# Hybrid decoder trunk on one core: the SBUF addresses of the weight, activation and scratch tiles moved off multiples of 1,024 bytes

## The reference

```python
h = rms_norm(x, norm_w)
proj = h @ w_in                          # 2048 x (3072+1024+8+8+512+256+64+1024+2048+2048)
# mixer A, gated DeltaNet, 8 heads of 128: conv + SiLU + L2 norm on q, k; chunked delta rule
o_a = rms_norm(gated_delta_rule_chunked(q, k, v, g, beta), gdn_norm_w) * silu(z_a)
# mixer B, latent attention, 8 heads: low-rank q and kv, rotary key, causal softmax
o_b = causal_block_attention(q_full, k_full, v_b, scale) * silu(z_b)
merged = sigmoid(gate_a) * (o_a @ proj_a) + sigmoid(gate_b) * (o_b @ proj_b)
out = rms_norm(x + merged @ w_out, final_norm_w)
```

## The kernel before

| Tile | Before | Rest | After the change | Rest |
|---|---|---|---|---|
| const | 16,512 | 128 | 65,664 | 128 |
| param | 19,648 | 192 | 68,800 | 192 |
| gball | 21,056 | 576 | 74,304 | 576 |
| rec (x_c, state) | 21,312 | 832 | 226,112 (slot 30) | 832 |
| w_raw, w_hi, w_lo | 23,552 | 0 | 16,512 | 128 |
| krope, cs | 72,704 | 0 | 70,208 | 576 |
| h_hi, h_lo (and y) | 76,800 | 0 | 74,560 | 832 |
| c_hi, c_lo (and m_hi, m_lo) | 142,336 | 0 | 140,096 | 832 |
| slots | 166,912 | 0 | 164,672 | 832 |

## Time and profile before

### The profile page before, as it was taken

How to read it: one execution, slowest core, us unless ns; L and a number is a source line. 1 busy time by engine, 2 the same in 40 slices (tenths; PEclk the granted TensorE clock), 3 DMA queues, 4 the chain that set the end, 5 groups by cost and what they waited for, 6 DMA issues and landing times.

```text
span 1589.7 us, 21230 instructions
## 1 busy us (share of the span) xinstructions
PE 1546.0 (97%) x7380; PEld 1268.6 (80%) x7380; DVE 724.4 (46%) x1320; ACT 569.1 (36%) x1027; POOL 94.8 (6%) x166
## 2 busy tenths in 40 slices
PE   5999999899999999999999999999999999999997
PEld 2777887688888888888888888888887788888886
DVE  6626565654353453452552542543533544533332
ACT  4336566533333332333332432333333322222222
POOL 3000000000000000100000000000011110100000
PEclk8999999999999999999999999999999999999999
DMA  5222323221331321322322223313234544362222
GB/s 208 97 96 80 133 106 125 100 93 54 114 110 66 132 106 66 132 79 99 125 77 100 100 79 106 119 53 115 82 114 154 182 145 156 134 238 106 91 94 106
DMA packets 32390, 177.67 MB, mean 112 GB/s; under 512 B 4896, under 2 KB 4896, under 8 KB 16496
## 3 DMA queue, kind: packets, MB, share of 16 engines
q1 hardware_dynamic: 19872, 134.09, 23.8%
q0 software_dynamic: 12496, 43.30, 7.5%
HBM read 156.37 MB, written 21.00 MB: 112 GB/s over the span
## 4 chain that ended last, share of the span: by engine, by line
PE 94%; DVE 3%; DMA 1%; ACT 1%; issue 0%; SPq 0%; POOL 0%; DVEq 0%; ACTq 0%; POOLq 0%
PE bank L233 23%; PE bank L235 23%; PE bank L234 22%; PE bank L1414 4%; PE bank L1413 4%; PE bank L1415 4%; PE bank L1196 3%; PE bank L1186 3%; PE bank L1204 1%; PE bank L1348 1%; PE bank L1205 1%; PE bank L1133 1%; DMA slots<-in_xt 1%; DVE slots L712 1%; DVE h_lo L717 1%; DMA o_in<-o_scratch 1%
## 5 line engine op out<-in xcount | busy, mean ns | idle before, releaser
L233 PE MATMUL bank<-h_hi,w_hi 128*128 128x512 f32 x1520 | 633.0, 416 | 14.5 <-DVE h_lo L717 8.7
L235 PE MATMUL bank<-h_hi,w_lo 128*128 128x512 f32 x1520 | 596.9, 393 | 0.0
L234 PE MATMUL bank<-h_lo,w_hi 128*128 128x512 f32 x1520 | 595.7, 392 | 0.0
L225 DVE TENSOR_TENSOR w_lo<-w_raw,w_hi 128x512 fp32r<-128x512 f32 x468 | 306.1, 686 | 205.2 <-ACT w_hi L218 205.2
L233 PEld LDWEIGHTS bank<-h_hi,w_hi 128*128 128x128 f32 x1520 | 287.8, 189 | 84.1 <-issue 12.4
L234 PEld LDWEIGHTS bank<-h_lo,w_hi 128*128 128x128 f32 x1520 | 288.1, 190 | 64.1 <-issue 9.7
L235 PEld LDWEIGHTS bank<-h_hi,w_lo 128*128 128x128 f32 x1520 | 287.1, 189 | 63.4
L218 ACT CAST w_hi<-w_raw 128x512 fp32r<-128x512 f32 x476 | 271.9, 618 | 89.0 <-PE bank L1415 86.6
L884 DVE COPY_PREDICATED slots<-lmask,bank 128x512 f32<-128x512 uint8 x48 | 35.1, 731 | 157.2 <-issue 157.2
L1413 PE MATMUL bank<-w_hi,m_hi 128*128 128x512 f32 x256 | 99.6, 389 | 0.0
L1414 PE MATMUL bank<-w_lo,m_hi 128*128 128x512 f32 x256 | 99.6, 389 | 0.0
(11 more groups left out here) (197 smaller groups left out, 1395.9 us busy)
## 6 DMA issues: line engine op xcount, KB each, us to landing
w_raw<-in_stream SPq DMA_DIRECT2D x119, 1024.0 KB, 4.8
gate_scratch<-slots POOLq DMA_DIRECT2D x32, 256.0 KB, 4.4
gate_in<-gate_scratch POOLq DMA_DIRECT2D x32, 256.0 KB, 2.9
slots<-in_xt SPq DMA_DIRECT2D x8, 512.0 KB, 11.2
qk_scratch<-slots POOLq DMA_DIRECT2D x16, 256.0 KB, 2.3
slots<-qk_scratch POOLq DMA_DIRECT2D x16, 256.0 KB, 2.9
slots<-gb_scratch POOLq DMA_DIRECT2D x16, 256.0 KB, 4.5
o_scratch<-slots POOLq DMA_DIRECT2D x16, 256.0 KB, 2.5
```

What stands on the lines that cost most here:

```text
L225: on.tensor_tensor(w_lo[b][:, sl], w_raw[b][:, sl], w_hi[b][:, sl].bitcast(F32), ALU.subtract).then_inc(lo_done, 1)
L233: nc.tensor.matmul(dst, a_hi, b_hi, start=start, stop=False)
L234: nc.tensor.matmul(dst, a_hi, b_lo, start=False, stop=False)
L235: return nc.tensor.matmul(dst, a_lo, b_hi, start=False, stop=stop)
```

## The change

The weight tiles are placed first, at the base, without rounding to 1,024 bytes; the constants follow them; `rec` has no place of its own any more and is the 31st slot, as many slots as fit being placed (31). The slice `small` takes the rest of that slot, 128 columns instead of 64, of which the same columns are used. After the change no tile starts at a multiple of 1,024 bytes or of 256; all start at multiples of 64. Nothing else is edited, and every engine has the same instructions in the same order with the same waits; only the name `rec` gives way to `slots` in the operands.

```diff
+        w_raw = [place(f"w_raw{b}", [P, TILE], F32) for b in range(2)]
+        w_hi = [place(f"w_hi{b}", [P, TILE], F32R) for b in range(2)]
+        w_lo = [place(f"w_lo{b}", [P, TILE], F32R) for b in range(2)]
         const = place("const", [P, N_CONST], F32)
         param = place("param", [P, N_PARAM], F32)
         lmask = place("lmask", [P, 7, P], U8, 1)
-        gball = place("gball", [P, NH, 8], F32)
-        rec_t = place("rec", [P, 3 * P + 64], F32)
-
-        at[0] = (at[0] + 1023) // 1024 * 1024
-        w_raw = [place(f"w_raw{b}", [P, TILE], F32) for b in range(2)]
-        w_hi = [place(f"w_hi{b}", [P, TILE], F32R) for b in range(2)]
-        w_lo = [place(f"w_lo{b}", [P, TILE], F32R) for b in range(2)]
         krope = place("krope", [P, SEQ], F32)
         cs = place("cs", [P, SEQ], F32)
+        gball = place("gball", [P, NH, 8], F32)
         h_off = at[0]
...
-        n_slots = 30
+        n_slots = (nc.sbuf_top - at[0] - 64) // (SEQ * 4)
         slots = place("slots", [P, n_slots, SEQ], F32)
-        assert at[0] <= nc.sbuf_top, (at[0], nc.sbuf_top)
+        assert n_slots >= 31, n_slots
...
-        rec = rec_t[:]
+        rec = slot(30)
         x_c, v_new, state = rec[:, 0:P], rec[:, P:2 * P], rec[:, 2 * P:3 * P]
-        small = rec[:, 3 * P:3 * P + 64]
+        small = rec[:, 3 * P:4 * P]
```

## The result

The changed kernel takes 1,617.17 us (median of 2 runs, 1,614.84 to 1,619.5) against 1,591.22: a ratio of 1.0163, 95% interval 1.0128 to 1.0197. It is slower by 26 us: less than 2%, but the interval is clear of 1, and the time is above the 1,606 us at which the stated range ended. The forecast of no change was wrong.

What follows compares the result with a forecast made beforehand. The prediction took TensorE's dense matmul spacing as the bound; TensorE, VectorE, ScalarE and DMA terms of 0 left the span at 1,589.7 us, plus 1.6 us outside it, giving 1,591.3 us, range 1,587 to 1,606.

Steps and rivals of the forecast that it cites:

- What bounds the kernel: Whole span: TensorE, busy for 1,546.0 of 1,589.7 us, bounds it through dense matmuls started 0.2262 us apart.
- the price of 5.57 us a nanosecond: All 5,568 dense matmuls: 1 ns more or less between their starts changes the time by 5.57 us.
- TensorE, moving operand at the rest 832: value taken 0 ns: Matmuls moving a tile at 832 modulo 1,024: no added cost, 0 ns each, read from float32 rows of 128 columns.
- the value 0 for the stationary operand at the rest 128: TensorE's weight loads from tiles at 128 modulo 1,024: no added cost, from loads of 190 against 189 ns.
- the 0.04 us of room beside the load: Weight loads beside the running matmul: growth up to 0.23 - 0.19 = 0.04 us would cost nothing.
- A: Every dense matmul: long float32r streams off a 1,024-byte boundary lose 11 ns more, 61 us, 1,652 us in all; chance 0.08.
- B: Dense matmuls: a clash of moving and stationary reads goes away, saving 11 ns each, 61 us, to 1,530 us; chance 0.04.
- C: All engines and transfers: small costs add up to 14.5 us, 1,605.8 us, or 1,622 us growing by columns; chance 0.12.
- The other terms: VectorE, ScalarE and DMA: each taken as 0, no added cost at the new addresses.
- The transfers: DMA: weights still land in 4.8 us a tile, arrival of `x` stays 10.8 us; worst reading 7.0 us more.
- What would show it: Signs of no change: 619 matmuls in 140 us in the output projection, named durations kept; wrong if spacing changed over 1 ns.

Runs made afterwards that it cites:

- e7_h32: The kernel before with 32 bytes of padding ahead of `h`, same instructions in the same order; 1,617.04 us, ratio 1.0157 to the kernel before.
- e3_all64: The kernel before with everything from the weights on shifted together by 64 bytes; 1,591.17 us, ratio 0.9997 to the kernel before.
- e1_w0_h832: The kernel before with weights kept at multiples of 1,024 bytes and `h`, `c`, `m`, `y`, `slots` at rest 832; 1,601.51 us, ratio 1.0078.
- e11_wlo_hlo64: The kernel before with `w_lo` and `h_lo` both moved by 64 bytes, `w_hi`, `h_hi`, `c`, `m`, `slots` kept at multiples of 256; 1,608.41 us, ratio 1.0099.

## Why the prediction was wrong

**What bounds the kernel: right, with one step too short.** TensorE's spacing was the place to look: 23.3 us of span are 4.2 ns on average over 5,568 products. But the price of 5.57 us a nanosecond took the spacing of the merge, 0.2262 us, for all of them, and a nanosecond in the merge is not one in the heads: 6.7 ns a product in the merge, 1.9 in the output projection, 4.1 in the heads of the changed kernel. In e7_h32 both stages lose 6.4 to 6.6 ns, for which the price list would give 36 us; the kernel lost 25.

**"TensorE, moving operand at the rest 832: value taken 0 ns": this is the step that failed**, with the value 0 for the stationary operand at the rest 128. Taken together they measured 4.2 ns a product, 23.3 us. Both were read from float32 products and from the length of a weight load, and the earlier trace rows, and carried over to float32r products of 512 columns. The loads did keep their 189 ns; the spacing grew all the same, and the 0.04 us of room beside the load did not protect it. Those rows were true and remain true, at other differences too: L1225, L1242 and L1233 of before had pairs that differed by 64 or 192, the changed kernel has them at 0, and they take 272 ns in both. They could not show the effect. The prediction named the gap ("no row here shows a float32r operand off a multiple of 512") and then took the mean over rows that did not close it.

**The question was also put wrongly.** The prediction asked of each tile whether its address was good, one operand at a time. The runs show that no address is good or bad alone: e3_all64 has every tile off and loses nothing, e1_w0_h832 has the weights on their boundary and loses 0.78%.

**The rivals.** A (slower, with float32r at 512 columns as the place) had the right place and the right kind of instruction, but a price of 11 ns a product, 1,652 us; the measured 4.2 ns is below the 5.7 from which it decides. B asked whether the two reads clash when both stand at multiples of 1,024 and are free of it at 832 and 128. A relation of the two reads is what it is, with the sign reversed: agreement is the fast state. C with its cost growing by columns gave 22 us on TensorE and 1,622 us. Its size was nearly right by luck: the 128-column rows show no cost that could be scaled up. The stated range left this part out.

**The other terms: right.** VectorE and ScalarE keep 685 and 618 ns for the split at the new offsets, and their totals to 1 us. The transfers: the chain goes through another of the transfers of `x` in the new trace, so its piece compares badly, but the chain's first L712 starts at 23.31 us before and the same instruction (L709) at 23.60 after, so the whole arrival is 0.3 us later at most; and the DMA issues of the changed kernel read

```profile
w_raw<-in_stream SPq DMA_DIRECT2D x119, 1024.0 KB, 4.8
...
slots<-in_xt SPq DMA_DIRECT2D x8, 512.0 KB, 10.9
```

against 4.8 and 11.2 us before. Of the partly used first transaction that the Trainium skill describes ("DMA: Bandwidth & Descriptors", "How a descriptor splits into AXI transactions"; its words are about what a transaction reads, while here it is the written address that moved) the trace shows nothing at 128 bytes past a multiple of 256 for the weights and 64 past one for `x`.

**What would show it.** The prediction said that it would be wrong if the spacing of the dense matmuls changed by more than 1 ns, and it did. Of its other signs only the count of matmuls moved. L1413's duration is 388 ns for the 389 that were named, the load of `w_lo` 189, L928 (now L925) 347 for 348, and the weights land in 4.8 us. The count was to be taken in the output projection, where the loss is mildest (526 in 120 us instead of 531); the merge shows it plainly, 601 instead of 619.

## What to carry to other kernels

Where float32r products of 512 columns with a fresh weight load for each are the bound, as here, place the stationary and the moving tiles, hi and lo parts alike, at the same offset modulo 256 bytes; the tiles need no boundary of their own, and 64 bytes of padding in the right place were worth 1.6% here. When a repacking of SBUF moves the time, look at the count of matmuls in a stretch without stops before and after: 619 against 601 in 140 us cannot be seen in busy shares, which are 97% in both pages. A row clears a change only for the instruction that the row shows, in its data type and its length.

## What the runs showed of the hardware that I had not expected

The speed of a float32r stream depends on where the two tiles of its products stand relative to each other. The Trainium skill ("TensorE: Matmul & The Clock Gate", section "Step-by-step: what each phase is for") says that TensorE has two independent SBUF read ports and that loading the next weights does not take read bandwidth from the running matmul. In this kernel the load's recorded time never changes (189 ns in the dense products of the kernel before and of the changed one), which agrees, but the spacing of the float32r products is 226 ns when the tiles agree modulo 256 and 228 to 233.5 ns when they do not, which it does not explain.

The difference 192 is a milder case, 228.1 and 228.4 ns, in the two stages and two kernels in which it occurred; its mirror image 64 gave 232.9 and 232.6. Why the sign counts is open. That the cost comes from the load beside the stream is not shown: e11_wlo_hlo64 gives every load a stream of its own residue, and the merge stays slow.

The three products of a group need not share the loss evenly. In the output projection of the changed kernel they take 388, 392 and 394 ns where each took 389, although all three have the same difference modulo 256.
